# Norms of a two-layer decoder step: weight folded into the first multiplication, bias into the low part, biased value made later

## The reference

```python
def layer_norm(x, g, b):
    xf = x.astype(jnp.float32)
    mu = jnp.mean(xf, axis=-1, keepdims=True)
    var = jnp.mean(jnp.square(xf - mu), axis=-1, keepdims=True)
    y = (xf - mu) * lax.rsqrt(var + LN_EPS) * g.astype(jnp.float32) + b.astype(jnp.float32)
    return y.astype(x.dtype)

def sq_relu_mlp(x, w_up, w_down):
    return jnp.square(jax.nn.relu(x @ w_up)) @ w_down
...
        yp = layer_norm(ALPHA * yp + mp, ln_g[layer, 0], ln_b[layer, 0])
        ys = layer_norm(ALPHA * ys + ms, ln_g[layer, 0], ln_b[layer, 0])
        yp = layer_norm(ALPHA * yp + sq_relu_mlp(yp, w_up[layer], w_down[layer]), ln_g[layer, 1], ln_b[layer, 1])
        ys = layer_norm(ALPHA * ys + sq_relu_mlp(ys, w_up[layer], w_down[layer]), ln_g[layer, 1], ln_b[layer, 1])
```

## Time and profile before

| | |
|---|---|
| median of 3 runs | 1395.46 us (1393.62 to 1395.48) |
| the profiled execution's own time | 1396.67 us |
| its span, first to last instruction | 1395.1 us |
| mean granted TensorE clock | 0.988 |
| TensorE matmul busy | 1349.7 us (97%) |
| TensorE weight load busy | 1286.0 us (92%) |
| VectorE busy | 722.7 us (52%) |
| ScalarE busy | 506.0 us (36%) |
| GpSimd busy | 395.2 us (28%) |
| DMA, mean rate | 89 GB/s |

### The profile page before, as it was taken

One profiled execution on the slowest core, in us unless ns is written; L12 is line 12 of the kernel. 1 busy time (PEld: TensorE's weight loads), 2 busy tenths in 40 slices (PEclk: granted clock), 3 DMA queues, 4 the chain that ended last, 5 costly groups with the idle time before them and its releaser, 6 DMA issues. The chain is left out here.

```text
span 1395.1 us, 27563 instructions
## 1 busy us (share of the span) xinstructions
PE 1349.7 (97%) x11310; PEld 1286.0 (92%) x11310; DVE 722.7 (52%) x1390; ACT 506.0 (36%) x1014; POOL 395.2 (28%) x467
## 2 busy tenths in 40 slices
PE   5999999999999999999999999999999999999996
PEld 5999999999999999999899766668999999999996
DVE  3425966774343343446789655553674343333435
ACT  3322236454031231234442467775453131230311
POOL 3013535652010010137534371025651010110102
PEclk9999999999999999999999899999999999999998
DMA  5351251213313131304331154212303222222201
GB/s 159 100 143 61 91 188 65 71 52 121 122 61 121 62 121 61 122 8 99 99 62 37 33 170 129 62 44 79 122 19 123 102 87 96 93 89 99 84 31 62
DMA packets 87101, 123.87 MB, mean 89 GB/s; under 512 B 24338, under 2 KB 42206, under 8 KB 86944
## 3 DMA queue, kind: packets, MB, share of 16 engines
q1 hardware_dynamic: 82048, 107.00, 24.0%
q0 software_dynamic: 4928, 15.10, 3.6%
HBM read 115.62 MB, written 8.57 MB: 89 GB/s over the span
## 5 line engine op out<-in xcount | busy, mean ns | idle before, releaser
L1063 PE MATMUL ps<-xh,ring_lo 128*128 128x260 f32 (+2 forms) x2496 | 504.6, 284 | 0.0
L1063 PEld LDWEIGHTS ps<-xh,ring_lo 128*128 128x128 f32 (+2 forms) x2496 | 383.6, 187 | 1.5 <-ACT big L1679 0.4
L1063 PE MATMUL ps<-xl,wr 128*128 128x260 f32 x1568 | 351.8, 283 | 6.1 <-DVE xl L2179 3.8
L1063 PE MATMUL ps<-xh,wr 128*128 128x260 f32 x1568 | 353.4, 284 | 1.4 <-DVE ring_lo L2081 1.0
L1063 PEld LDWEIGHTS ps<-xl,wr 128*128 128x128 f32 x1568 | 255.6, 188 | 7.8 <-DVE xl L2179 5.0
L1063 PEld LDWEIGHTS ps<-xh,wr 128*128 128x128 f32 x1568 | 256.3, 188 | 3.5 <-ACT att L1716 1.4
L866 POOL TENSOR_TENSOR att<-att 128x520 f32<-128x520 f32 (+1 forms) x80 | 77.3, 967 | 548.5 <-DVE att L2105 521.5
L2081 DVE TENSOR_TENSOR ring_lo<-ring,wr 128x1024 fp32r<-128x1024 f32 (+1 forms) x144 | 192.0, 1336 | 60.2 <-ACT wr L1679 60.1
L1063 PE MATMUL ps<-hh,wr 128*128 128x260 f32 x1024 | 222.1, 283 | 0.0
L1063 PE MATMUL ps<-hh,ring_lo 128*128 128x260 f32 x1024 | 221.8, 283 | 0.0
L1063 PE MATMUL ps<-hl,wr 128*128 128x260 f32 x1024 | 221.7, 283 | 0.0
(11 more groups left out here) (356 smaller groups left out, 1581.1 us busy)
## 6 DMA issues: line engine op xcount, KB each, us to landing
ring<-in_w_up SPq DMA_DIRECT2D x16, 2048.0 KB, 7.9
ring<-in_w_down SPq DMA_DIRECT2D x16, 2048.0 KB, 7.9
ring<-in_w_in_e SPq DMA_DIRECT2D x9, 1024.0 KB, 6.8
ring<-in_w_in_e SPq DMA_DIRECT2D x2, 2048.0 KB, 8.7
ring<-in_w_out_e SPq DMA_DIRECT2D x2, 2048.0 KB, 9.4
ring<-in_w_in_o SPq DMA_DIRECT2D x16, 256.0 KB, 4.9
ring<-in_cache_kv POOLq DMA_DIRECT2D x32, 128.0 KB, 2.4
ring<-in_w_out_o SPq DMA_DIRECT2D x8, 512.0 KB, 7.9
```

The lines of the kernel that those rows point to most:

```text
L1063: last = pe.matmul(bank(g, half)[0:width(g), 0:H2], w[:, k, :], x[:, k, cols(half)], start=first, stop=final)
```

## The change

Weight and reciprocal deviation are multiplied in together in `normed`, so that `xT` holds the weighted value without its bias. ScalarE makes `xh` from it with the bias alone. VectorE makes all eight low parts, each in one instruction: value plus bias minus high part. GpSimd's `x_low` is gone, and so are ScalarE's `affine` into `xT` and VectorE's affine step. The value with its bias, which the next residual needs, is made by ScalarE in the next stage, over all 520 columns at once (`shifted`), and VectorE's residuals there wait for it.

In the MLP stages (`n_ln` 0 and 2, so norms 0 and 2) the dummies of the head are gone, the sums of half 1 stand behind tile 1, and the steps of half 1 on all engines stand one tile later. The stage behind norm 1 keeps its dummies and its places.

```diff
             def head(n_ln, g):
...
-                keep_busy(3, 14 if n_ln == 1 else 5)
+                if n_ln == 1:
+                    keep_busy(3, 14)
...
                 def first_tile(k):
-                    if k == 2:
+                    if k == 2 and n_ln == 1:
                         keep_busy(3, 10)
...
-                    if i == 0:
+                    if i == (0 if n_ln == 1 else 1):
                         norm_sums(n_ln, 1)
...
             def mlp(layer, g):
                 n_ln = 2 * layer
-                moments(n_ln, 1)
                 for j in range(KD):
                     hidden(layer, g + j, 0, j, 0)
                     if j == 0:
+                        moments(n_ln, 1)
+                    if j == 1:
                         deviation(n_ln, 1)
-                    if 1 <= j <= 4:
-                        scaled(n_ln, 1, (2 * j - 2, 2 * j - 1))
+                    if 2 <= j <= 5:
+                        scaled(n_ln, 1, (2 * j - 4, 2 * j - 3))
                 for j in range(KD):
                     hidden(layer, g + j, 0, j, 1)
+                    shifted(n_ln, j)
...
+            def shifted(n_ln, m):
+
+                act.wait_ge(sm["xl_v"], KD * (2 * n_ln + 1) + m + 1)
+                act.activation(xT[:, m, :], xT[:, m, :], ACT.Identity,
+                               bias=colT[:, 32 + KD * n_ln + m:33 + KD * n_ln + m]).then_inc(sm["x_ready"], 1)
...
                     act.wait_ge(sm["cen_v"], KD * (2 * n_ln + half) + m + 1)
-                    affine(XH[n_ln], n_ln, m, half).then_inc(sm["x_hi"], 1)
-                    act.wait_ge(sm["x_hi"], KD * (2 * n_ln + half) + m + 1)
-                    if m in XT_ACT:
-                        affine(xT, n_ln, m, half).then_inc(sm["x_ready"], 1)
+                    c = cols(half)
+                    act.activation(XH[n_ln][:, m, c], xT[:, m, c], ACT.Identity,
+                                   bias=colT[:, 32 + KD * n_ln + m:33 + KD * n_ln + m]).then_inc(sm["x_hi"], 1)
...
                 w_hi_ahead(g)
+                if 4 <= idx < 4 + KD:
+                    shifted(1, idx - 4)
...
-            def residual(g0, m, half, scale):
+            def residual(g0, m, half, scale, n_in=None):
 
                 tile_done(g0 + m, half)
+                if n_in is not None:
+                    dve.wait_ge(sm["x_ready"], KD * n_in + m + 1)
...
                     dve.wait_ge(sm["cen_p"], KD * (2 * n_ln + half) + m + 1)
-                    dve.tensor_tensor(x, x, rs[:, c], ALU.mult).then_inc(sm["cen_v"], 1)
+                    dve.scalar_tensor_tensor(x, x, colT[:, KD * n_ln + m:KD * n_ln + m + 1], rs[:, c], ALU.mult,
+                                             ALU.mult).then_inc(sm["cen_v"], 1)
...
             def x_low(n_ln, half, m):
                 c = cols(half)
-                if m in XT_ACT:
-                    dve.wait_ge(sm["x_ready"], xr(n_ln, half) + XT_ACT.index(m) + 1)
-                else:
-                    dve.wait_ge(sm["x_hi"], KD * (2 * n_ln + half) + m + 1)
-                    link(dve.tensor_scalar(xT[:, m, c], xT[:, m, c], colT[:, KD * n_ln + m:KD * n_ln + m + 1],
-                                           colT[:, 32 + KD * n_ln + m:33 + KD * n_ln + m], ALU.mult, ALU.add))
-                dve.tensor_tensor(XL[n_ln][:, m, c], xT[:, m, c], XH[n_ln][:, m, c].bitcast(F32), ALU.subtract).then_inc(sm["xl_v"], 1)
+                dve.wait_ge(sm["x_hi"], KD * (2 * n_ln + half) + m + 1)
+                dve.scalar_tensor_tensor(XL[n_ln][:, m, c], xT[:, m, c], colT[:, 32 + KD * n_ln + m:33 + KD * n_ln + m],
+                                         XH[n_ln][:, m, c].bitcast(F32), ALU.add, ALU.subtract).then_inc(sm["xl_v"], 1)
```

More of the change, by code:

```diff
@@ L66 @@
 MISC = 60
-XT_ACT = (1, 3, 5, 7)
-XL_POOL = (1, 3, 5)
-XL_DVE = (0, 2, 4, 6, 7)
 SPLIT_NORMS = (0, 1, 2)
@@ L356, in coming @@
             return at(g + NW)
-        def xr(n_ln, half):
-            return len(XT_ACT) * (2 * n_ln + half)
         def w_raw(u):
@@ L835, in norm @@
             def norm(n_ln, g0):
-                for i, (m, half) in enumerate(norm_order(n_ln)):
+                for m, half in norm_order(n_ln):
                     if m:
@@ L848, in split_y @@
                 pool.tensor_tensor(xl[:, k, :], y[:, at + k, :], xh[:, k, :].bitcast(F32), ALU.subtract).then_inc(sm["y_split"], 1)
-            def x_low(n_ln, half, ms):
-                c = cols(half)
-                for m in ms:
-                    pool.wait_ge(sm["x_ready"], xr(n_ln, half) + XT_ACT.index(m) + 1)
-                    pool.tensor_tensor(XL[n_ln][:, m, c], xT[:, m, c], XH[n_ln][:, m, c].bitcast(F32), ALU.subtract).then_inc(sm["xl_p"], 1)
             def hidden(layer, g, c, j, half=None):
@@ L872, in mlp @@
                     hidden(layer, g + j, 0, j, 0)
-                    if j < 2:
-                        centre(n_ln, 1, range(4 * j, 4 * j + 4))
-                    if 3 <= j < 6:
-                        x_low(n_ln, 1, (XL_POOL[j - 3],))
+                    if 1 <= j < 3:
+                        centre(n_ln, 1, range(4 * j - 4, 4 * j))
                 for j in range(KD):
@@ L1078, in x_lo_here @@
             def x_lo_here(n_ln, half):
-                n = 2 * SPLIT_NORMS.index(n_ln) + half
-                def ready(k):
-                    if k in XL_POOL:
-                        pe.wait_ge(sm["xl_p"], len(XL_POOL) * n + XL_POOL.index(k) + 1)
-                    else:
-                        pe.wait_ge(sm["xl_v"], len(XL_DVE) * n + XL_DVE.index(k) + 1)
-                return ready
+                return lambda k: pe.wait_ge(sm["xl_v"], KD * (2 * SPLIT_NORMS.index(n_ln) + half) + k + 1)
             def head(n_ln, g):
                 n = HEADS[g]
-                keep_busy(3, 14 if n_ln == 1 else 5)
+                if n_ln == 1:
+                    keep_busy(3, 14)
                 hi_here = x_hi_here(n_ln, 0)
                 def first_tile(k):
-                    if k == 2:
+                    if k == 2 and n_ln == 1:
                         keep_busy(3, 10)
@@ L1746, in mlp @@
                     norm(1, g - KD)
-            def affine(out, n_ln, m, half):
-                c = cols(half)
-                return act.activation(out[:, m, c], xT[:, m, c], ACT.Identity, scale=colT[:, KD * n_ln + m:KD * n_ln + m + 1],
-                                      bias=colT[:, 32 + KD * n_ln + m:33 + KD * n_ln + m])
+            def shifted(n_ln, m):
+                act.wait_ge(sm["xl_v"], KD * (2 * n_ln + 1) + m + 1)
+                act.activation(xT[:, m, :], xT[:, m, :], ACT.Identity,
+                               bias=colT[:, 32 + KD * n_ln + m:33 + KD * n_ln + m]).then_inc(sm["x_ready"], 1)
             def moments(n_ln, half):
@@ L2115, in mlp @@
                 n_ln = 2 * layer
-                variance(n_ln, 1)
                 for j in range(KD):
@@ L2119, in mlp @@
                     if j == 0:
+                        variance(n_ln, 1)
+                    if j == 1:
                         inverse(n_ln, 1)
-                    if j <= 4:
-                        normed(n_ln, 1, NORMED[n_ln][j])
-                        x_lows(n_ln, 1, LOWS[n_ln][j])
+                    if 1 <= j <= 5:
+                        normed(n_ln, 1, NORMED[n_ln][j - 1])
+                        x_lows(n_ln, 1, LOWS[n_ln][j - 1])
                 for j in range(KD):
@@ L2133, in mlp @@
                             for half in range(2):
-                                residual(g, m, half, scale)
+                                residual(g, m, half, scale, n_ln if c == 0 else None)
                             w_lo_ahead(g + m)
@@ L2159, in normed @@
                     dve.wait_ge(sm["cen_p"], KD * (2 * n_ln + half) + m + 1)
-                    dve.tensor_tensor(x, x, rs[:, c], ALU.mult).then_inc(sm["cen_v"], 1)
+                    dve.scalar_tensor_tensor(x, x, colT[:, KD * n_ln + m:KD * n_ln + m + 1], rs[:, c], ALU.mult,
+                                             ALU.mult).then_inc(sm["cen_v"], 1)
             def x_lows(n_ln, half, ms):
                 for m in ms:
-                    if m in XL_DVE:
-                        x_low(n_ln, half, m)
+                    x_low(n_ln, half, m)
             PAIRS = ((0, 1), (2, 3), (4, 5), (6, 7))
@@ L2184, in norm @@
                 for m, half in norm_order(n_ln):
-                    residual(g0, m, half, scale)
+                    residual(g0, m, half, scale, 1 if n_ln == 2 else None)
                     if (m, half) == (KD - 1, 0):
```

6 lines of the change are left out of this document (1 added, 5 removed).

## The result

| | before | after |
|---|---|---|
| median of 4 runs beside each other | 1394.54 us (1393.52 to 1395.48) | 1379.59 us (1379.26 to 1380.64) |
| ratio, 95% interval | | 0.9898 (0.9884 to 0.9912) |
| profiled execution | 1396.67 us | 1379.6 us |
| its span | 1395.1 us | 1378.0 us |
| mean granted TensorE clock | 0.988 | 0.991 |

Faster by 15.0 us; forecast were 10.6 us, and 1384.9 us (1380.5 to 1391.5).

The account below looks back on a forecast made before the run. TensorE, 97% busy, was taken to lose time only in waits and unneeded work. Terms −4.9 − 4.7 − 1.6 + 0.6 = −10.6 us, against the median of 1395.46, gave 1384.9 us, range 1380.5 to 1391.5.

Parts of the forecast that it names:

- part 4: Norm 1, dummies kept: low parts and sums come sooner, 1.6 us gained (0 to 3.0).
- Part 1: Heads of norms 0 and 2: removing dummies saves up to 3.5 us each, if the low parts are there.
- Part 2: VectorE, 16 instructions a half for 17, the new one 490 ns: last low part about 278.1 us, no wait in tile 0.
- Part 3: Norms 0 and 2, sums one tile later: new wait of 1.1 us each, weight 7's wait gone; gains 4.9 and 4.7.
- Part 5: Biased value made later by ScalarE: nothing in the MLPs, +0.6 us (0 to 1.3) in the odd projections.
- Waits move: Rival, 12%: dummies filled time TensorE would wait anyway; only 3 us gained in all, 1392.4 us.
- Port freed: Rival, 15%: without GpSimd's 18 subtractions VectorE runs mostly undisturbed, all waits vanish; −14.8 us, 1381 us.
- The clock falls: Rival, 5%: without dummies TensorE idles at the heads and its clock drops to the lower level; +7.8 us, 1403 us.

Follow-up runs that it names:

- e1: The kernel before with only the dummy matmuls taken out of the heads behind norms 0 and 2; 1393.86 us, ratio 1.0009.
- e3: The changed kernel with only the dummies put back at the heads of norms 0 and 2; 1384.10 us, ratio 0.9925.
- e2: The changed kernel with the dummies back and half 1's sums and following steps back behind tile 0; 1382.30 us, ratio 0.9918.
- e4: The changed kernel, still without dummies, with half 1's sums and following steps back behind tile 0; 1386.94 us, ratio 0.9951.
- e8: The changed kernel with VectorE's low part of the weight put behind the first hidden tile's own low part; 1377.36 us, ratio 0.9882.
- e12: The changed kernel with ScalarE's eight biased values in the odd projection made four tiles later; 1380.32 us, ratio 0.9902.
- e5: The changed kernel run once more, unaltered, for a second profile and more times; 1379.80 us, ratio 0.9904.
- e11: The changed kernel with the weight's column given again as scale to ScalarE's high-part activation, beside the bias; 1380.07 us, ratio 0.9899.
- e13 to e16: Four single runs, unaltered, kernel before and changed kernel in turn, for third and fourth profiles: 1390.96, 1381.02, 1392.02, 1379.41 us.
- e10: The changed kernel with norm 1's dummies deleted too; 1383.49 us, ratio 0.9921.

## Why the prediction was right or wrong

The miss of 5.3 us against the forecast splits into 0.9 (before's median beside the changed kernel was 1394.54 us, not 1395.46), 1.3 (the change gave 11.9 us and not 10.6) and 3.1 (the medians lie 15.0 us apart where the norms account for 11.9).

Two steps failed. Among the terms it is norm 1's (part 4): put at 1.6 us and at 3.0 at most, it gave 3.5, since I read that stage only as far as its sums. The sum hides it in part by luck: norms 0 and 2 gave 8.4 us and not 9.6, and the odd projection 0.0 where I had +0.6. But with the terms as measured the sum would still have been 1383.6 us, inside the range. What took the time out of it is the base: the range held the costs of the change alone and put at nothing, without a reason, how much the two medians differ for all that the change leaves as it is, 0.9 and 3.1 us here.

- **Part 1, dummies.** Near in the sum, wrong in the split. The stretches went from 30.0 to 25.8 us and 29.8 to 25.6, 4.2 us less each, where I said 4.9 and 4.7. But the dummies are not worth 3.2 us by themselves: nothing without the arithmetic (e1), 1.5 to 1.7 us with all the rest in place (e3). The three pieces of the change hang together: arithmetic 1.95 us (e2), then dummies nothing (e4 against e2, norm 2: 27.76 and 27.79), then the shift 2.2 us.
- **Part 2, VectorE.** Right. The two lines of the new instruction in the changed kernel, against the earlier trace rows:

```profile
L2143 DVE SCALAR_TENSOR_TENSOR xT<-xT,colT,att x48: 476/840/980, 257.8 to 1014.1; 128x260 f32<-128x260 f32 x48
L2157 DVE SCALAR_TENSOR_TENSOR xl<-xT,colT,xh x48: 473/480/977, 261.7 to 1016.4; 128x260 fp32r<-128x260 f32 x48
```

  480 ns where 490 were taken, up to 980 in collision, and no wait for a low part in norms 0 and 2. Its last low part ended 1.3 us after the last residual tile (273.62 + 1.37 less 273.67), which I had put at 1.9.
- **Part 3, the sums.** The new wait was forecast at 1.1 us and measured 1.58 and 1.37. What was wrong in it: GpSimd's last sum was taken undisturbed, 0.74 us; it took 1.71 us, because the shift lets VectorE's next weight run beside it (e8). The wait for weight 7 is gone, as said. Without that collision the excess is 0.8 us, not 1.8, and the wait 0.60 us (e8), less than my 1.1: the undisturbed sums would have come sooner than I had put them, and the two errors partly cancel.
- **Part 4, norm 1.** Mis-sized: −3.5 us in place of −1.6, beyond its end of −3.0. TensorE's rows behind norm 1 in the changed kernel, against the earlier trace rows:

```profile
646.45 3.29 PE L1007 MATMUL ps<-ones,ident 128*128 128x128 f32 x28
...
655.26 0.33 PE L1045 MATMUL ps<-xl,wr 128*60 128x260 f32 x1 [0.84 <-DVE xl L2157]
...
657.54 1.04 PE L1007 MATMUL ps<-att,meanM 128*128 128x260 f32 x4
```

  The sums stand 11.1 us behind the first dummy and no longer 13.3: 2.2 us, within the bounds given. Left out was what follows. In the kernel before, the second half's pass of this stage waited as well,

```profile
678.39 0.45 PE L1063 MATMUL ps<-xl,wr 128*60 128x260 f32 x2 [0.17 <-DVE xl L2179]
680.29 0.45 PE L1063 MATMUL ps<-xl,wr 128*60 128x260 f32 x2 [0.26 <-DVE xl L2179]
```

  and the sums ran at the low clock. From the sums to the first transpose it took 23.6 us and now 22.4. I had stopped reading at the sums. How much of the 3.5 us is the clock: e1, whose norm 1 is before's code but whose clock stayed up there, shows 44.97 us in its one profile, so 1.4 us are the clock and 2.1 the earlier low parts and the waits. Why the clock stays up here in the changed kernel, in four of four profiles, isn't shown.
- **Part 5, the biased value.** Hidden in the MLPs, as said. In the odd projection the step starts 0.6 us later, as said (a wait of 3.21 us where it was 2.61), and costs nothing: 91.3 us before and after. What was wrong was to carry a later start through to the chain's end. In the earlier trace rows the instruction took 2.16 us, long beside the 1.55 us of the changed kernel, and ended 0.28 us after GpSimd's weight, as in e12. GpSimd's weight in the kernel before:

```profile
699.02 2.40 POOL L813 TENSOR_TENSOR ring_lo<-ring,wr 128x1024 fp32r<-128x1024 f32 x1 [4.93 <-ACT wr L1679]
```

  Its end was cover for half a microsecond. That VectorE is held by the port it shares with GpSimd is my reading; the rows show only that the two ends go together.
- **The base.** The sum was set against 1395.46 us, the median of three runs, and the range took in the costs of the change alone. The attention, which the change leaves as it is, scatters between 192 and 199 us over 18 profiles, the start-up between 252.4 and 255.5. In the profile that I read both stood near their upper end. A range needs such a term, of at least 2 to 3 us on each side. Whether the 3.1 us between medians and norms are all scatter isn't settled, since only the profiled runs show their stretches. The distance varies with the runs: in e5's the changed kernel lies 14.2 us below before; e11 and e12, whose norms take as long as its own, lie 13.6 and 13.3 us below; the single times of e13 to e16 are 11.3 us apart in the mean.
- **The rivals.** *Waits move* was true of the kernel before (e1), and with the new arithmetic as long as the sums stood behind tile 0 (e4 against e2, norm 2); with the sums behind tile 1 it was not (e3). *Port freed* is nearest in number; its mechanism holds for part of VectorE's work, while the multiplication's median is still 840 ns, 928 before, and by its own number the waits for the sums should have vanished, which stayed at 1.58 and 1.37 us. *The clock falls* needs less than I thought: two waits of 1.6 and 2.7 us (e1), one of 3.4 (e4). The changed kernel's longest wait at these heads is 1.58 us, and its clock stayed up in all four profiles.

## What to carry to other kernels

A dummy matmul is free while its engine would wait anyway, and it may hold the clock for what follows; so judge it by leaving it out, and again after each change of what it covers (e1, e3, e10). When work is moved behind a wait, look at what its absence lets run beside the others: the shift that gained 2.2 us gave 1.0 back because VectorE now reached a weight while GpSimd made the last sum. And read a stretch through to where the next one starts alike, not to the first landmark.

## What was not expected of the hardware

- Behind waits of nearly the same length (3.42 and 3.21 us, in the same kernel and the same code) the clock fell in one place and not in the other; against e2, where it stayed up, the fall cost 2.4 us in norm 0. In the kernel before, norm 1's clock fell in four of four profiles; with only norms 0 and 2 changed (e1) it did not, in the one profile there is.
- A column as ScalarE's scale, next to the column that is its bias, costs 0.09 us: 605 ns with both and 512 with the bias alone, at 260 elements. The Trainium skill (ScalarE: Activation LUTs, What ACT_TABLE_LOAD costs) gives 93 ns for each such operand, and the rows agree; I had not looked for it. VectorE's new instructions took 473 to 480 ns undisturbed, the one with an immediate 417; since that one reads an input from PSUM and these both from SBUF, how much of the 60 ns is the column's isn't shown.
- The attention's time differs by 7 us between profiles, though its instructions are the same in all kernels (192.1 to 199.0), with the granted clock between 0.99 and 0.95.
